# Idle products in the tail's waits, a square root moved on ScalarE, the output projection by chunks, and two openings rearranged

## The reference

```
first block, twice:
  proj = x @ w_in                      -> u, v, ssm input, q, k, av, gates
  a = u * (tril(w_s) @ layer_norm(v) + b_s)
  b = diagonal state-space scan (32 groups x 64 states), gelu, GLU
  c = attention of 8 heads
  merged = g0 * (a @ w_a) + g1 * (b @ w_b) + g2 * (c @ w_c)
  x = layer_norm(2**0.5 * x + merged @ w_out)
  x = layer_norm(2**0.5 * x + (silu(x @ w1) * (x @ w3)) @ w2)
second block, once, with 256 context tokens ahead of the 256:
  mod = silu(c) @ w_ada + b_ada        (12 column blocks of 512)
  h = layer_norm(ctx), layer_norm(x), each scaled and shifted by mod
  mixer: h @ w_in_2, convolutions, mLSTM and RWKV-7 heads, both directions
  x = layer_norm(2**0.25 * x + g1 * (mixed @ w_out_2))
  h2 = layer_norm(x) scaled and shifted by mod
  route each token: 1 of 4 groups, 2 of its 8 experts (hidden width 512)
  x = layer_norm(2**0.25 * x + g2 * experts(h2))
```

## Time and profile before

| | us |
|---|---|
| median of three runs | 2134.33 |
| the profiled execution | 2128.23 |
| its span | 2126.2 |
| layers of the first block, about | 0 to 1045 |
| second block up to the WKV scan, about | 1045 to 1360 |
| tail: norms, routing, first expert, about | 1586 to 1684 |
| loop over pairs of experts, about | 1684 to 2104 |

### The profile page before, as it was taken

The page is one execution under the profiler, slowest core; times in us unless marked ns, Lnnn a source line. Parts: engine busy times, 40 slices in busy tenths (PEclk is TensorE's granted clock), DMA queues, the critical chain, the costliest instruction groups (busy, mean ns, idle before and its releaser), DMA issues.

```text
span 2126.2 us, 33504 instructions
## 1 busy us (share of the span) xinstructions
PE 2045.5 (96%) x13831; PEld 1380.5 (65%) x13831; DVE 852.7 (40%) x1551; ACT 471.5 (22%) x881; POOL 250.8 (12%) x233
## 2 busy tenths in 40 slices
PE   8999999999999999999899999999997999999996
PEld 6678868864768877885354665799985444444442
DVE  1794220001379222000348856545456333233324
ACT  2255100000416300000132125433322111111111
POOL 2783000000378100000000001100000000000000
PEclk9999999999999999999989999999997899999998
DMA  7332544444533254435631333400011999999992
GB/s 243 119 119 100 198 148 143 145 159 141 181 119 119 100 198 150 143 105 196 224 134 40 119 104 136 159 3 3 3 46 37 378 419 420 413 414 415 421 414 123
DMA packets 138697, 385.37 MB, mean 181 GB/s; under 512 B 16935, under 2 KB 64399, under 8 KB 127441
## 3 DMA queue, kind: packets, MB, share of 16 engines
q1 hardware_dynamic: 138577, 383.61, 48.6%
HBM read 382.54 MB, written 1.05 MB: 180 GB/s over the span
## 4 chain that ended last, share of the span: by engine, by line
PE 45%; DVE 2%; ACT 2%; issue 1%; DMA 0%; DVEq 0%; ACTq 0%
PE psum L1297 9%; PE psum L2876 9%; PE psum L2044 8%; PE psum L2900 5%; PE psum L2809 3%; PE psum L2931 2%; PE psum L1496 1%; PE psum L2460 1%; ACT arena L1654 1%; PE psum L2113 1%; PE psum L2062 1%; PE psum L1319 1%; PE psum L1312 0%; DMA ring<-in_w_ada_dram 0%; PE psum L2888 0%
## 5 line engine op out<-in xcount | busy, mean ns | idle before, releaser
L383 PE MATMUL psum<-arena,ring 128*128 128x256 f32 x1728 | 382.3, 380 | 1.0 <-ACT arena L666 1.0
L383 PEld LDWEIGHTS psum<-arena,ring 128*128 128x128 f32 x1728 | 324.1, 189 | 55.8 <-issue 8.6
L602 PE MATMUL psum<-arena,ring 128*128 128x256 f32 (+1 forms) x1536 | 306.8, 361 | 3.6 <-ACT arena L657 3.6
L602 PEld LDWEIGHTS psum<-arena,ring 128*128 128x128 f32 x1536 | 270.5, 189 | 39.6 <-issue 2.3
L2044 PE MATMUL psum<-arena 64*64 64x64 f32 (+1 forms) x4320 | 180.1, 237 | 2.7 <-issue 1.5
L2044 PEld LDWEIGHTS psum<-arena 64*64 64x64 f32 x4320 | 171.9, 134 | 4.7 <-issue 2.7
L666 ACT ACTIVATE arena<-psum 128x512 f32<-128x512 f32 (+2 forms) x100 | 54.4, 563 | 506.8 <-PE psum L602 264.1
L629 PE MATMUL psum<-ring,arena 128*128 128x512 f32 x352 | 151.7, 592 | 0.0
L1297 PE MATMUL psum<-arena,ring 128*128 128x512 f32 (+2 forms) x432 | 142.2, 489 | 0.0
L1067 DVE TENSOR_TENSOR arena<-arena,psum 128x512 f32<-128x512 f32 x22 | 15.2, 690 | 289.2 <-PE psum L602 289.2
L1297 PEld LDWEIGHTS psum<-arena,ring 128*128 128x128 f32 (+1 forms) x432 | 80.6, 187 | 61.4 <-issue 55.8
(11 more groups left out here) (418 smaller groups left out, 2568.4 us busy)
## 6 DMA issues: line engine op xcount, KB each, us to landing
ring<-in_w_in_dram SPq DMA_DIRECT2D x29, 2048.0 KB, 8.2
ring<-in_ffn_w_dram SPq DMA_DIRECT2D x46, 1024.0 KB, 5.8
arena<-in_ex_gate_dram SPq DMA_DIRECT2D x15, 2048.0 KB, 11.1
arena<-in_ex_up_dram SPq DMA_DIRECT2D x15, 2048.0 KB, 15.6
arena<-in_ex_down_dram SPq DMA_DIRECT2D x15, 2048.0 KB, 15.0
ring<-in_ex_gate_dram SPq DMA_DIRECT2D x14, 2048.0 KB, 8.2
ring<-in_ex_up_dram SPq DMA_DIRECT2D x14, 2048.0 KB, 12.7
ring<-in_ex_down_dram SPq DMA_DIRECT2D x14, 2048.0 KB, 16.3
```

Of the source, the lines that this page charges most:

```text
L383: ins = pe.matmul(bank[:, j, :], w[:, kc, c * P:(c + 1) * P], moving[:, kc, :], start=kc == 0, stop=kc == k - 1)
L602: ins = pe.matmul(bank[:, j, tokens], both[:, i * DC + kc, j * P:(j + 1) * P], K.xT[:, kc, tokens], start=kc == 0, stop=kc == DC - 1)
```

## The change

It has no new arithmetic that reaches the output. Part by part:

- *Layer front.* The first five parameter loads get a semaphore of their own, `dma_vrows`. TensorE turns the parameter rows before the SSM projection; ACT runs the Exp and Sin steps before it empties the ssm banks; of u only the first half stands before the turning of B, the second after it; q's first half moves behind the first states' inputs. DVE waits for the remaining 24 loads just before it multiplies B.
- *Output projection.* The wait for `merged` is taken per piece in the first bank. The turning of x1's first tile goes into the middle of the last bank's products.
- *From the first block to the second.* Only in the last layer: the useless turning for the next layer is dropped; the rows of parameters are turned before the last two down units; ACT does copies, silus and the strip before the last norm; DVE normalises the context before that norm, and each token tile right after its last norm. Two of four early ada units are loaded to a place of their own (`K.early`, over tiles dead by then), so all later units move up two places in the ring. POOL fills most of its constants earlier. In the mid phase the tokens are turned tile by tile, and the gates' weights are gathered between context and tokens.
- *Tail.* ACT takes the root of the second tile's first norm before it copies the gate rows. `idle_products` puts products of constants, which nobody reads, ahead of five waits of TensorE: 2 and 5 ahead of `x4` of the two tiles, 2 and 4 ahead of the two `route`, 5 ahead of `one_chosen`.

```diff
@@ layer_tensor
         tokens("v", 1, [1])
-        project("ssm", 2)
-
-        pe.wait_ge(K.sem["dma_params"], K.count("dma_params", l))
+        pe.wait_ge(K.sem["dma_vrows"], K.count("dma_vrows", l))
         pe.wait_ge(K.empty(("vec", 0)), K.empty_count(("vec", 0), l))
         bank = K.bank(("vec", 0))
         pe.wait_ge(K.sem["dt_row"], K.count("dt_row", l))
         pe.transpose(bank[:, 0:P], K.vrows, ident).then_inc(K.full(("vec", 0)), 1)
+        project("ssm", 2)
+        pe.wait_ge(K.sem["dma_params"], K.count("dma_params", l))
...
-        project("u", 0)
+        project("u", 0, [0])
         pe.wait_ge(K.sem["ssm_bbar"], K.count("ssm_bbar", l))
...
-        project("q", 3, [0])
+        project("u", 0, [1])
...
         state_inputs(0)
+        project("q", 3, [0])
+        state_inputs(1)
         project("q", 3, [1])
-        state_inputs(1)
-        project("k", 4, [0])
         state_inputs(2)
-        project("k", 4, [1])
+        project("k", 4)
...
-        pe.wait_ge(K.sem["merged"], K.count("merged", l))
...
                 for kc in range(DC):
+                    if (tt, hf) == (0, 0) and kc % 2 == 0:
+                        pe.wait_ge(K.sem["merged"], K.count("merged", l, kc // 2 + 1))
+                    if (tt, hf) == (1, 1) and kc == DC // 2:
+                        turn_tile("x1", "x1T", 0)
...
+        if l == DEPTH - 1:
+            pe.wait_ge(K.sem["dma_vec"], K.count("dma_vec"))
+            for i in range(2):
+                pe.wait_ge(K.empty(("next", i)), K.empty_count(("next", i), l))
+            pe.transpose(K.bank(("next", 0))[:, 0:P], K.vrows2, ident).then_inc(K.full(("next", 0)), 1)
...
@@ layer_scalar
+        if l == DEPTH - 1:
+            mid_open_scalar(act, K, l)
         for tt in range(TT):
...
+            if tt == 0 and l == DEPTH - 1:
+                second_std(act, K, 1)
@@ layer_vector
+                if l == DEPTH - 1 and name == "x2":
+                    dve.wait_ge(K.sem[done], K.count(done, l, 2 * TT + 2 * tt + 2))
+                    second_norm(1 + tt)
...
+        if l == DEPTH - 1:
+            dve.wait_ge(K.empty(("f3", FFN_UNITS - 1)), K.drained_count(("f3", FFN_UNITS - 1), l))
+            dve.wait_ge(K.sem["dma_ctx"], K.count("dma_ctx"))
+            second_norm(0)
         norm("x2", "f2", 2, "x_in")
@@ mid_sync
-    for c in (0, 1, 2):
-        sp.wait_ge(K.used_up(("ada", c)), K.free_count(("ada", c)))
+    for c, landed in enumerate(("dma_ada_0", "dma_ada_1")):
         weights = rows(A["w_ada_2"])[:, :, c * BANK:(c + 1) * BANK]
-        sp.dma_start(K.slot_like(("ada", c), weights), weights).then_inc(K.landed(("ada", c)), 16)
+        sp.dma_start(K.early[:, c], weights).then_inc(K.sem[landed], 16)
+    for kind, c in mid_units()[0:3]:
+        sp.wait_ge(K.used_up((kind, c)), K.free_count((kind, c)))
...
+def second_std(act, K, n):
+
+    act.wait_ge(K.sem["nrm_var"], K.count("nrm_var", 0, n + 1))
+    std, var = ((K.nrm_std[:, 0, :], K.nrm_mv[:, 0, :, 1]) if n == 0 else
+                (K.nrm_std[:, 1, n - 1:n], K.nrm_mv[:, 1, n - 1:n, 1]))
+    act.activation(std, var, ACT.Sqrt).then_inc(K.sem["nrm_std"], 1)
...
+def idle_products(pe, K, key, n):
+
+    pe.wait_ge(K.empty(key), K.empty_count(key))
+    for _ in range(n):
+        pe.matmul(K.bank(key), K.ident, K.g_rows[:, 0, 0:BANK], start=True, stop=True)
@@ tail_tensor, pair_tensor
     def token_tile_turned(tt):
+        idle_products(pe, K, ("h2T", 2 * tt), (2, 5)[tt])
         pe.wait_ge(K.sem["x4"], K.count("x4", 0, tt + 1))
...
+    idle_products(pe, K, ("h2", 0, 0), 2)
...
     pe.wait_ge(K.sem["route"], K.count("route", 0, 1))
...
+    idle_products(pe, K, ("h2", 0, 0), 4)
     pe.wait_ge(K.sem["route"], K.count("route", 0, 2))
...
+    idle_products(pe, K, ("xg1", 0), 5)
     pe.wait_ge(K.sem["one_chosen"], K.count("one_chosen"))
-    pe.wait_ge(K.empty(("xg1", 0)), K.empty_count(("xg1", 0)))
@@ tail_scalar
         act.activation(K.x_std2[:, tt:tt + 1], K.x_mv2[:, tt, 1:2], ACT.Sqrt).then_inc(K.sem["x3_std"], 1)
+        if tt == 1:
+            gate_rows(1)
         act.wait_ge(K.sem["x4_var"], K.count("x4_var", 0, tt + 1))
...
-        if tt == 0:
-            gate_rows(1)
```

More of the change, by code:

```diff
@@ L641, in layer_tensor @@
         down(W2_UNITS - 2, [(1, hf) for hf in range(2)]).then_inc(K.used_up(("w2", W2_UNITS - 2)), 1)
-        for i in range(2):
-            pe.wait_ge(K.sem["x_in"], K.count("x_in", l, 2 * TT + i + 1))
-            pe.wait_ge(K.empty(("next", i)), K.empty_count(("next", i), l))
-            turn(("next", i), 0, i)
+        if l < DEPTH - 1:
+            for i in range(2):
+                pe.wait_ge(K.sem["x_in"], K.count("x_in", l, 2 * TT + i + 1))
+                pe.wait_ge(K.empty(("next", i)), K.empty_count(("next", i), l))
+                turn(("next", i), 0, i)
         for hf in range(2):
@@ L1093 @@
 BIG = 1e30
+EARLY = 2
 LATE = [4, 5, 10, 11, 6, 7, 8, 9]
@@ L1101, in mid_units @@
 def mid_units():
-    return [("ada", c) for c in range(4)] + [("w2in", c) for c in (7, 3, 4, 2, 1, 0, 5, 6)] + [("ada", c) for c in LATE]
+    return [("ada", c) for c in range(EARLY, 4)] + [("w2in", c) for c in (7, 3, 4, 2, 1, 0, 5, 6)] + [("ada", c) for c in LATE]
 def mid_groups():
-    keys = [("bvec", 0)]
+    keys = [None] * (len(layer_groups()) % BANKS)
     keys += [("mod_row", i) for i in range(4)] + [("mod", 0)]
@@ L1124, in mid_closes @@
 def mid_closes():
-    closes = {("mod_row", i): ("ada", i) for i in range(4)} | {("late_row", i): ("ada", c) for i, c in enumerate(LATE)}
+    closes = {("mod_row", i): ("ada", i) for i in range(EARLY, 4)} | {("late_row", i): ("ada", c) for i, c in enumerate(LATE)}
     closes |= {("lg", 0): ("w2in", 7)}
@@ L1303, in strips @@
     def strips(c, key, unit):
-        pe.wait_ge(K.landed(unit), K.landed_count(unit))
-        w = K.weights(unit, DC, BANK)
+        if unit in (("ada", 0), ("ada", 1)):
+            landed = ("dma_ada_0", "dma_ada_1")[unit[1]]
+            pe.wait_ge(K.sem[landed], K.count(landed))
+            w = K.early[:, unit[1]]
+        else:
+            pe.wait_ge(K.landed(unit), K.landed_count(unit))
+            w = K.weights(unit, DC, BANK)
         pe.wait_ge(K.empty(key), K.empty_count(key))
@@ L1338, in mid_tensor, with turned @@
     ins.then_inc(K.full(("mod", 0)), 1)
[L1339 to L1348 removed]
+    def turned(s, q, tt):
+        bank = K.bank(("hT", s, q)).rearrange("p (k n) -> p k n", k=2)
+        for j in range(2):
+            ins = pe.transpose(bank[:, j, tt * P:(tt + 1) * P], K.nrm[:, 1 - s, tt, (2 * q + j) * P:(2 * q + j + 1) * P], ident)
+        return ins
+    pe.wait_ge(K.sem["nrm"], K.count("nrm", 0, 1))
+    for q in range(4):
+        pe.wait_ge(K.empty(("hT", 0, q)), K.empty_count(("hT", 0, q)))
+        turned(0, q, 0)
+        turned(0, q, 1).then_inc(K.full(("hT", 0, q)), 1)
+    for tt in range(TT):
+        pe.wait_ge(K.sem["nrm"], K.count("nrm", 0, 2 + tt))
+        for q in range(4):
+            if tt == 0:
+                pe.wait_ge(K.empty(("hT", 1, q)), K.empty_count(("hT", 1, q)))
+            ins = turned(1, q, tt)
+            if tt == 1:
+                ins.then_inc(K.full(("hT", 1, q)), 1)
     for s in range(2):
@@ L1691, in mid_gpsimd @@
     link = Chain(K.pool_done, K.pool_base)
-    pool.wait_ge(K.sem["x_in"], K.count("x_in", DEPTH))
-    for tile in (K.g_row, K.neg_G, K.neg_m, K.gate_w):
+    pool.wait_ge(K.full(("f3", FFN_UNITS - 1)), K.full_count(("f3", FFN_UNITS - 1), DEPTH - 1))
+    for tile in (K.neg_G, K.neg_m, K.gate_w):
         pool.memset(tile, 0.0).then_inc(link.sem, 1)
```

169 lines of the change are left out of this document (83 added, 86 removed).

## The result

The changed kernel takes 2096.31 us in the median (four executions, 2094.62 to 2099.61) against 2132.88 us before (2130.91 to 2136.81): a ratio of 0.9828, 95% interval 0.9809 to 0.9848, so 36.6 us less. The forecast was 2104.2, with 2096 to 2118 as its range; the time lies 0.3 us inside its lower edge.

What follows compares the result with a forecast made beforehand. TensorE was taken as the bound, busy 2045.5 of 2126.2 us. Layer front 4.8, output projection 3.2 and 1.8, opening 14.8 and tail 5.5 sum to 30.1; 2134.3 less 30.1 gives 2104.2 us, range 2096 to 2118.

Steps and rivals of the forecast that it cites:

- The rival in which loads or DVE bound it: Second block's opening: loads or DVE bound it, taking half of the 14.8 us gain; 2111.6 us, chance 0.07.
- A rule that speaks against it: Opening's transposes: the skill says full clock does not engage for transposes; the forecast held that the earlier trace disagrees.
- the rival's 1.7 us in the gate products: Opening: clock falls in the transposes, first gate products lose 1.7 us; 3.6 in all, 2107.8 us, chance 0.03.
- firm part: Tail: the second tile's first norm gets its square root 5.3 us earlier, directly after its variance.
- Cost 4.0: Tail: lateness that the products of constants cause before the second route and first expert's choice, 4.0 us.
- 0.2 of those 3: Tail: of the products' net clock gain of 3 us only 0.2 was counted, as the clock was expected to fall again.
- Just fits: Tail: five products before the second tile's turning end about 1627, before x4 comes about 1631.4.
- 1.3 late: Tail: four products before the second route leave TensorE free about 1642.3, the route known about 1641.
- 2.7 late: Tail: five products before the first expert's choice end at 1651.7, the choice comes about 1649.
- 7.0: Tail: us that the products of constants save by full clock in later work, where the clock does not fall.
- Products in the way: Tail: products at half clock push back the route's and choice's products; gain 5.5 becomes -2.5, 2112.2 us, chance 0.13.
- The slower side: From the first block's end to the expert loop: half clock throughout, eating 14 of the opening's 14.8; 2140.7 us, chance 0.05.

Runs made afterwards that it cites:

- p1_front: The kernel before with the layer front's edits alone: 2120.89 us against 2128.56, ratio 0.9968.
- t1_again: The changed kernel once more, unedited, timed beside before: 2094.43 us against 2129.29, ratio 0.9840.
- p4_tail: The kernel before with the tail's edits alone, 18 products of constants and the moved root: 2122.45 us, ratio 0.9982.
- t4_few: The changed kernel with 2, 5, 0, 0, 2 products of constants in the five places: 2091.36 us, ratio 0.9809.
- r1_root: The kernel before with only the square root moved ahead of the gate rows on ACT: 2126.31 us, ratio 0.9984.
- t2_none: The changed kernel without any product of constants, their five waits for a free bank kept: 2093.53 us, ratio 0.9825.
- r2_noroot: The changed kernel with the square root put back behind the gate rows, its 18 products kept: 2103.60 us, ratio 0.9878.

## Why the prediction was right, and where it was not

**Layer front.** Right: 5.3 us in p1_front's trace for 4.8, and each time on the way (44.4 for 45, 49.86 for 50). No row of before gave the landing of the five loads; they were there.

**Output projection and x1's first tile.** Right: 4.8 for 5.0. The 1.6 of L591 became 0.3 of a new releaser, so 1.3 was got; the gate's step gave 1.1 where 0.9 was its wait.

**Opening.** Right in mechanism, 2 us too small: 18.8 us were reckoned between the end of the FFN's products and the gate (the list of signs has 18.6 for the same, from a gain of 14.3 where the sum has 14.8), 16.76 came. The 32 transposes took 3.69 for 4.2, the four ada units and their columns 11.5 for 11.9, and the emptyings cost one wait of 2.0 in place of 2.7; none of the covers gave way. The rival in which loads or DVE bound it is out (16.76 in nine traces).

**A rule that speaks against it.** The transposes L1388 ran at full clock in the profiled execution of the changed kernel, 3.69 us for the 32 that had taken 6.05. Two stretches of it, columns as in the earlier trace rows:

```profile
1030.00:1050.00 20.00, 18.17 (x136) 10.11 (x135) 14.41 (x35) 6.76 (x15) 0.53 (x1) 1.00 0.97 347
1050.00:1060.00 10.00, 9.81 (x19) 4.28 (x20) 0.94 (x2) 0.00 (x0) 0.00 (x0) 0.83 0.41 148
```

Behind them the clock did fall for 3.4 us: the first 16 passes of the gate took 8.81 us. In t1_again the same 16, behind the same transposes and the same 2.0 us of wait, took 7.12, at a clock of 1.00:

```profile
1046.00:1060.00 14.00, 12.00 (x54) 7.21 (x54) 5.65 (x16) 3.86 (x8) 0.00 (x0) 1.00 0.69 253
```

So the rival's 1.7 us in the gate products came in one execution and not in the other; of the nine traces with this opening four have 8.8 us and five 7.1. Whether the transposes or the wait behind them brought it is open. The Trainium skill ("TensorE: Matmul & The Clock Gate", Part 4: PE-mode transpose) has transposes not counted as busy; a clock of 1.00 through t1_again's stretch, 3.7 us of nothing but transposes and 2.0 idle, gives that rule no support here.

**Tail.** The sum was right in size in two traces (5.5 forecast; 4.9 in t1_again, 4.8 in p4_tail, both the shortest executions of their kernels) and not in the first profile (0.15), and its firm part was all of it: the root alone gives 5.8. The step that failed is "Cost 4.0" with "0.2 of those 3", the account of the products of constants. Four terms of it:

- "Just fits", for the five ahead of the second tile. x4 came 13.0 us behind the dense products, as reckoned, but in the first profile the gate rows ended at 9.6 for 8.7, and the five took 5.25 us for 4.35: the turning is 1.5 us late there and in t1_again, 3.1 in t4_few. The root's move itself had taken most of the gap that they were to fill (6.8 to 1.9 in r1_root).
- "1.3 late", for the second route. It is 1.4 in t1_again, but 5.3 in the first profile: two products take 1.97 us at 2.4 GHz and 3.76 at 1.2, and 1.3 could hold for full clock alone.
- "2.7 late", for the choice. The gather starts 4.5 us behind its choice in t1_again and 4.4 in the first profile: ACT's emptying is waited for first, and the five behind it take 6.2 and 6.1 us, since they run in part at half clock. The very stretch for which they were added is the one in which they may run at half.
- "7.0", for what the clock gives back. The four savings that are listed add up to 8.7; without the gate rows' 1.8, which lie ahead of a wait, they are 6.9. Against t2_none, at 1.2 GHz for half of its tail, all of them together gave back less than the lateness cost.

So "net 0.2" for the products is in truth from about -1 to -5.5 us by execution. By the forecast's own sign (L2511 or L2818 late behind idle products by over 4 us) this part was wrong in both profiles, though the time came out in the range. The rival *Products in the way* named this mechanism, and its price (8 us worse than the forecast's tail) came in part: 5.3 in the first profile, 0.6 in the second.

**Sum and base.** 30.1 us were forecast. The two traces differ by 28.5 with the tail at its worst, and by 35.3 if the second profile of the changed kernel (2090.9) is taken; the medians by 36.6 and 34.9. What put the forecast 8 us too high was mostly its base: the median of the three executions that were shown was 2134.3, and 6.1 us of it over the profiled execution were carried over. In the 57 later executions of before the medians were 2128.6, 2129.3 and 2128.5, as the profiled one's 2128.2. From there 30.1 less is 2098. Of the rest the traces place 1.6 at the opening (a lead of 16.4 for 14.8) and 1.6 at the clock of the second layer. Told as a gain, 30.1 stands against 36.6 (32.4 to 40.7) in the first comparison and 34.9 (29.6 to 38.8) in t1_again's: too small against the one, inside the other, and what is left between them no trace places.

**The slower side** (half clock throughout) did not come: it would have wanted 20 us more of low clock, and the opening alone lost up to 20.5 of them.

## What to carry to other kernels

Look first for a short instruction that others wait for and that stands behind one which waits for another engine, and move it ahead: the root, 0.2 us long and moved up its queue, gave the tail's whole gain. Products that nobody reads are paid at the clock that they find: fill a gap only by what it holds at half clock, reckon the gap as the other edits leave it, keep the queue behind them free of what comes ready soon, and time the kernel without them before they are kept. A trace of one execution gives the waits; where the clock falls in light stretches, two traces of the same code show which differences are only that.

## What the hardware showed that was not expected

The same program on the same data has its clock fall in different places from execution to execution: before ranged over 13.5 us (0.6%) on one chip in step with its mean granted clock, 0.975 to 0.983. Without the products of constants the time was no longer (2093.5 against 2094.4). Its five executions lie within 0.7 us and those with all 18 within 7.8, but r2_noroot, with all 18 too, has its four within 0.3, so that products make a time unsteady is not shown. The tail of the changed kernel took 65.81 us at a mean clock of 0.87 and 61.04 at 0.94, that without products 60.32 at 0.75 (stretches of the three that begin within 0.1 us of the tail's start; columns as in the earlier trace rows):

```profile
1590.00:1656.00 66.00, 58.57 (x260) 35.51 (x260) 37.39 (x128) 17.58 (x39) 0.00 (x0) 0.87 0.58 230
```

```profile
1588.00:1650.00 62.00, 54.58 (x265) 33.43 (x265) 38.09 (x128) 17.57 (x39) 0.00 (x0) 0.94 0.62 246
```

```profile
1589.00:1650.00 61.00, 47.67 (x227) 35.22 (x228) 37.88 (x128) 17.46 (x39) 0.00 (x0) 0.75 0.63 250
```

The kernel with the lowest clock in the tail is the shortest of the three: a higher granted clock is worth only what it takes off the path, less what was issued to get it.
